# Moving eight gate shares from the first feed-forward product to the out-projection

## The reference

```
mod = silu(c) @ w_ada + b_ada                      # 1024 x 6144
shift1, scale1, gate1, shift2, scale2, gate2 = split(mod, 6)

h = rms_norm(x, g_pre_mix) * (1 + scale1) + shift1
proj = h @ w_in                                    # 1024 x 3584
mix = concat(short_conv(...), retention(...)) @ w_out
x = x + gate1 * rms_norm(mix, g_post_mix)

h = rms_norm(x, g_pre_mlp) * (1 + scale2) + shift2
f = square(relu(h @ w_fc1)) @ w_fc2                # 1024 x 4096, 4096 x 1024
x = x + gate2 * rms_norm(f, g_post_mlp)
```

## Time and profile before

| | us |
|---|---|
| median of 3 runs | 1420.72 |
| lowest, highest | 1420.6, 1421.6 |
| span of the profiled execution, first to last instruction | 1418.9 |
| around the span (median less span) | 1.8 |
| TensorE busy | 1408.4 (99%) |
| VectorE busy | 873.4 (62%) |
| ScalarE busy | 574.4 (40%) |
| DMA, mean rate | 111 GB/s |

### The profile page before, as it was taken

How to read it: one execution, slowest core, us unless ns; L and a number is a source line. 1 busy time by engine, 2 the same in 40 slices (tenths; PEclk the granted TensorE clock), 3 DMA queues, 4 the chain that set the end, 5 groups by cost and what they waited for, 6 DMA issues and landing times.

```text
span 1418.9 us, 20491 instructions
## 1 busy us (share of the span) xinstructions
PE 1408.4 (99%) x8186; PEld 1182.3 (83%) x8186; DVE 873.4 (62%) x1722; ACT 574.4 (40%) x1076; POOL 0.2 (0%) x4
## 2 busy tenths in 40 slices
PE   8999999999999999999999999999999999999998
PEld 7888888888888888888888888888888888888886
DVE  7887876543333335755466535422788889888645
ACT  6423355422333234542332323433445545556441
POOL 0000000000000000000000000000000000000000
PEclk9999999999999999999999999999999999999999
DMA  9556441353232324132332233132222222221221
GB/s 357 216 198 248 150 161 45 127 199 104 89 104 90 104 89 155 39 104 89 100 109 74 90 119 134 56 107 89 76 90 75 91 76 75 76 76 61 75 74 60
DMA packets 43726, 157.90 MB, mean 111 GB/s; under 512 B 4848, under 2 KB 5232, under 8 KB 43632
## 3 DMA queue, kind: packets, MB, share of 16 engines
q1 hardware_dynamic: 43344, 156.39, 31.8%
q10 hardware_dynamic: 288, 0.21, 0.1%
HBM read 154.48 MB, written 2.10 MB: 110 GB/s over the span
## 4 chain that ended last, share of the span: by engine, by line
PE 98%; DVE 1%; DMA 0%; ACT 0%; issue 0%; SPq 0%; DVEq 0%
PE PS L504 31%; PE PS L506 30%; PE PS L505 30%; PE PS L955 1%; PE PS L500 1%; PE PS L959 1%; PE PS L947 1%; PE PS L887 1%; PE PS L968 0%; DMA X<-in_x 0%; PE PS L940 0%; PE PS L892 0%; PE PS L915 0%; PE PS L762 0%; PE PS L782 0%; DVE RAW L1139 0%
## 5 line engine op out<-in xcount | busy, mean ns | idle before, releaser
L504 PE MATMUL PS<-HH,WH 128*128 128x512 f32 (+1 forms) x1072 | 415.3, 387 | 0.0
L506 PE MATMUL PS<-HH,WL 128*128 128x512 f32 (+1 forms) x1072 | 410.9, 383 | 0.0
L505 PE MATMUL PS<-HL,WH 128*128 128x512 f32 (+1 forms) x1072 | 410.6, 383 | 0.0
L1175 DVE TENSOR_TENSOR WL<-RAW,WH 128x1024 fp32r<-128x1024 f32 x216 | 262.6, 1219 | 71.4 <-ACT WH L2000 71.0
L2000 ACT ACTIVATE WH<-RAW 128x1024 fp32r<-128x1024 f32 x216 | 227.7, 1057 | 171.7 <-PE PS L506 129.9
L506 PEld LDWEIGHTS PS<-HH,WL 128*128 128x128 f32 x1072 | 201.5, 188 | 40.0
L504 PEld LDWEIGHTS PS<-HH,WH 128*128 128x128 f32 x1072 | 201.6, 188 | 39.4
L505 PEld LDWEIGHTS PS<-HL,WH 128*128 128x128 f32 x1072 | 201.7, 188 | 38.2
L504 PE MATMUL PS<-WH,ZH 128*128 128x512 f32 x400 | 155.9, 390 | 0.0
L506 PE MATMUL PS<-WH,ZL 128*128 128x512 f32 x400 | 155.6, 389 | 0.0
L505 PE MATMUL PS<-WL,ZH 128*128 128x512 f32 x400 | 155.6, 389 | 0.0
(11 more groups left out here) (278 smaller groups left out, 1763.3 us busy)
## 6 DMA issues: line engine op xcount, KB each, us to landing
RAW<-in_w_fc SPq DMA_DIRECT2D x64, 512.0 KB, 3.2
RAW<-in_hgrn_in SPq DMA_DIRECT2D x64, 512.0 KB, 3.2
RAW<-in_ada SPq DMA_DIRECT2D x44, 512.0 KB, 4.3
RAW<-in_pool_in SPq DMA_DIRECT2D x40, 512.0 KB, 3.3
RAW<-in_w_in SPq DMA_DIRECT2D x26, 512.0 KB, 5.1
RAW<-in_pool_out SPq DMA_DIRECT2D x16, 512.0 KB, 3.2
RAW<-in_hgrn_out SPq DMA_DIRECT2D x16, 512.0 KB, 3.2
RAW<-in_w_out SPq DMA_DIRECT2D x8, 512.0 KB, 3.8
```

Source lines behind the costliest of these rows:

```text
L504: e.matmul(out, wh, xh, start=first, stop=False)
L505: e.matmul(out, wh, xl, start=False, stop=False)
L506: return e.matmul(out, wl, xh, start=False, stop=last)
L1175: e.tensor_tensor(lo, raw(i), hi.bitcast(F32), ALU.subtract).then_inc(taken.sem, taken(i))
```

## The change

After the change the eight ada units 40 to 47 stand in `UNITS` behind the first four units of `w_out`, two behind each, and no longer one behind each of units 6 to 13 of `w_fc1`. The walk functions, the ring and everything else are the same code; what changes is where in every engine's program the shares, their loads and their neighbours' loads come.

```
                     ("hgrn_in", 64), ("hgrn_out", 16)):
         for i in range(n):
             out.append((name, i, True))
-            if name == "w_fc1" and 6 <= i < 14:
-                out.append(("ada", next(ada), False))
+            if name == "w_out" and i < 4:
+                out += [("ada", next(ada), False) for _ in range(2)]
```

## The result

| | before | after |
|---|---|---|
| median (runs) | 1420.66 (4) | 1426.87 (4) |
| lowest to highest | 1420.48 to 1421.6 | 1426.72 to 1427.4 |
| span of the profiled execution | 1418.9 | 1425.6 |

The ratio is 1.0043, with a 95% interval of 1.0031 to 1.0054: slower by 6.2 us. The forecast was 1426.6, slower by 5.9.

What follows compares the result with a forecast made beforehand. TensorE, busy 1408.4 of 1418.9 us, was taken as the bound, so any stall adds its full length. Terms 2.25 + 1.75 + 1.87 = 5.87 us on 1420.72 gave 1426.6 us; own range 1425.4 to 1427.8, eight-in-ten 1423.0 to 1429.0.

Steps and rivals of the forecast that it cites:

- What is removed is worth nothing: First feed-forward product: taking away eight shares and their loads gains 0, since TensorE never waited there.
- Column 26 hides two shares: Column 26: two shares of 2.58 us fit into VectorE's 2.95 us idle time before 185.00, costing nothing.
- The first stall: Column 27: two shares delay the second L1485, which frees bank 1, so TensorE's second out-projection product waits 2.25 us.
- Three round trips through the ring: Out-projection: three loads in turn each wait for VectorE to free a RAW slot, 3.5 us each from issue to landing.
- W3: Fourth out-projection unit: TensorE 4.00 us late, 1.75 beyond the bank, with a wait on L1175 of about 2 us.
- W6: Seventh out-projection unit: its late load makes TensorE 5.87 us late, 1.87 more, with a wait of about 2 us.
- three terms that add: Out-projection delay as a sum: 2.25 at the bank, 1.75 at the fourth unit, 1.87 at the seventh: 5.87 us.
- The clock: Claimed waits this short have not throttled TensorE; rival: a fall to 1.2 GHz adds 5.4 us, 1432, chance 0.03.
- Only the bank: Rival: out-projection transfers come in time, so only the 2.25 us at bank 1 stay: 1423.0, chance 0.09.
- S5's load: Sixth moved share: its load waits for the rest of the second out-projection unit, done 193.29, and lands 196.84.
- Absorbed: Rival: VectorE's idle time from 180 to 210 takes in the shares, nothing is late: 1420.7, chance 0.05.
- that rival: Slow landings: 5.0 us for each of three ring round trips, delay 10.4 us, 1431.1, chance 0.07.

Runs made afterwards that it cites:

- e7: Kernel before with only two shares moved, behind the first out-projection unit, six staying beside the first feed-forward product: 1420.55 us, -0.2 over before.
- e4: Kernel before with loads in place, its shares cut to 8 of 1024 columns, and eight stand-in VectorE instructions at the new places: 1424.42 us, 3.6 over before.
- e1: The changed kernel with VectorE freeing PSUM bank 1 in column 27 ahead of the third and fourth shares: 1427.96 us, 6.8 over before.
- e5: The changed kernel with the last three shares loaded into free places of Z instead of RAW ring slots: 1424.50 us, 3.3 over before.
- e3: The changed kernel with each share's VectorE instruction cut to 8 of 1024 columns, loads and slots kept: 1423.59 us, 2.4 over before.
- e10: The changed kernel with both the last three shares in places of Z and bank 1 freed first: 1423.55 us, 2.4 over before.
- e11: The changed kernel with VectorE freeing bank 1 in column 27 between the third and fourth shares: 1427.22 us, 6.1 over before.
- e6: The changed kernel with the eight shares placed one behind each of the eight out-projection units: 1425.71 us, 4.9 over before.
- e2: Kernel before with only two shares moved, behind the second out-projection unit, six staying beside the first feed-forward product: 1422.76 us, 1.6 over before.
- e9: Kernel before with only two shares moved, behind the fourth out-projection unit, six staying beside the first feed-forward product: 1421.54 us, 0.8 over before.

## Why the prediction was right

Point by point, by its own steps:

*What is removed is worth nothing.* Right: the feed-forward columns keep 5.44 us, and all later stages together differ by 0.03 us.

*Column 26 hides two shares.* Right in the trace (0.88 us idle left) and by e7, though the pair was taken at 2.58 us and cost 2.07.

*The first stall, 2.25 us at bank 1 on L1485.* It was 194.71 - 192.50 = 2.21 (TensorE would have gone on 0.68 after 191.82). e4 shows it without the loads, e1 shows that it can be taken away without a gain.

*Three round trips through the ring.* The landings took 3.8, 3.7 and 3.2 us, 10.7 together where three times 3.5 was counted. W3 was 4.33 us late (4.00 said), W6 5.78 (5.87), the pass 5.91. By e5 and e3 the slots cause it. The estimate of 3.2 us for each from the Trainium skill's fit ("DMA: Bandwidth & Descriptors", anatomy of one DMA) would have given 5.0; it fits the last of the three, not the other two.

*The form of the sum.* I wrote it as three terms that add. The number is right because their running total says how late the chain is at three points; it must not be read as three costs that can be repaired one by one. Without the bank 6.8 us stay (e1), without the slots 3.3 (e5), without both 2.4 (e10).

*The clock.* This is the statement that failed, though not the number. I wrote that waits as short as these have not lowered the clock, from the 1.9 us wait near the start. After the 2.05 us wait it fell to 1.2 GHz for some three microseconds. From the second product (194.71) to W1 (201.21) TensorE took 6.50 us where 4.76 is the price before (191.74 to 196.50): 1.74 us. By the trace it cost nothing in the changed kernel, as TensorE would else have spent them waiting for W3, whose rest was ready at 208.3 in any case: the wait before W3 that I foretold as about 2 us was 0.2. The one before W6, foretold as about 2 as well, was 0.6 for another reason: 1.45 us were added between W3 and W6 and not 1.87, and 0.6 of them already at W4 and W5. Where nothing follows that is late anyway, the fall is paid in full (e5). And in e1 and e11, where the wait is longest and comes last, the 30 matmuls from W3 to the second pass took 9.24 and 8.56 us, against 6.80 before and 8.38 in the change; of that, 1.0 and 0.4 us came on top of the chain. The wait that the statement was drawn from was 1.9 us, and the first stall was forecast as 2.25. The same wait at the start is 2.04 us in six other profiles, and three of them have a fall behind it (below). That the forecast held in spite of the fall is in part luck: in this kernel the loads behind it were later still.

*The rivals.* "Only the bank" needed S5's load to go out before the rest of W1 ended; it went out at 194.1, as that rest (192.84 + 1.22) ended. "Absorbed" needed the second L1485 by 190.9, or 191.7 with this profile's later start; it came at 193.98. The bursts did not slow the three loads that mattered to the 5.0 us of that rival.

What stays open: why the clock falls behind one wait and not behind another as long, the share of runs of the changed kernel in which it does, and why e6's median lies 0.8 us above what its one profile adds.

## What to carry to other kernels

Work moved off an engine beside a stage where the bottleneck never waits gains nothing, so the whole question is the place it goes to: find which of its successors there is wanted next, and how soon. A load that shares a small ring with the units around it can only be issued when an in-order engine has passed the unit five places before; if that engine then waits for it, each such pair costs a full round trip (3.2 to 3.8 us here), though the DMA engines are idle more than half of the time (share 0.44 from 190 to 200). Waits that follow each other on one engine can be one chain: take the first away and look whether the last moves before adding them up.

## What the hardware showed beyond expectation

- TensorE's clock fell from 2.4 to 1.2 GHz behind a wait of 2.05 us: in the change from 195.6 to 199.0 with the wait over at 194.71, in e5 just as the wait ended at 193.87. In e1 it fell at 207.0, within the wait of 4.50 us, and in e11 at 208.7, 0.6 us after that of 4.40. After waits of 1.98 (e4), 1.62 (e10), 1.54 (e6) and 1.52 us (e2) the profiled runs show no fall. e4 and e5 wait almost equally long at the same place, one without it and one with it.
- The length of the one wait does not decide it alone. Near the start TensorE waits 2.04 us for VectorE (on RAW, until 17.7 to 18.1) in the profiles of e1, e2, e4, e5, e9 and e10; from 18 to 30 the granted clock is 1.00 in e2, e5 and e10, and 0.86 in e1, e4 and e9, where it falls within 1.6 us of the wait's end. In the other profiles but that of the change this wait is 1.7 to 1.9 us and no fall follows; in the change it is 1.1 us and the clock had fallen before it, at 14.7. What decides stays open.
- The fall cost 1.7 us in e5, where nothing hid it.
- Three loads of 512 KB that each set out with the next one 0.3 to 0.4 us behind them landed after 3.8, 3.7 and 3.2 us; which it will be I could not tell from what is in flight.
